# Moving the low-part subtractions of the weights from GpSimd to VectorE, and starting SBUF areas at multiples of 512 bytes

## What is computed

```python
h = rms_norm(x); proj = h @ w_in                      # block 1: pooling + NSA attention
x = x + (gate_pool * y_pool + gate_nsa * y_nsa) @ w_out
h = rms_norm(x); gate_pre, val = split(h @ w_up)      # FFN, conv on the gate
x = x + (silu(causal_dwconv(gate_pre)) * val) @ w_down
h = rmsnorm(x); z = h @ w_in_2                        # block 2: gated delta rule + band attention
q, k, v = silu(causal_dwconv_2(qkv)); oa = gated_delta_rule(q, k, v, g, beta); ob = chunk_band_attention(...)
x = x + (sigmoid(ga) * (oa @ w_branch_a) + sigmoid(gb) * (ob @ w_branch_b)) @ w_out_2
u = causal_dwconv_2(h @ w_up_2) + b                   # FFN, conv on gate and value
x = rmsnorm(x + (silu(gate) * up) @ w_down_2)
```

## Time and profile before

| | us |
|---|---|
| median of 3 runs | 1731.11 (1723.51 to 1732.45) |
| the profiled execution | 1725.94 |
| its span in the trace | 1724.0 |
| busy PE / DVE / POOL / ACT | 1628.1 / 995.8 / 641.3 / 568.8 |

### The profile page before, as it was taken

The page is one execution under the profiler, slowest core; times in us unless marked ns, Lnnn a source line. Parts: engine busy times, 40 slices in busy tenths (PEclk is TensorE's granted clock), DMA queues, the critical chain, the costliest instruction groups (busy, mean ns, idle before and its releaser), DMA issues.

```text
span 1724.0 us, 21757 instructions
## 1 busy us (share of the span) xinstructions
PE 1628.1 (94%) x7872; PEld 1277.9 (74%) x7872; DVE 995.8 (58%) x1295; ACT 568.8 (33%) x906; POOL 641.3 (37%) x274
## 2 busy tenths in 40 slices
PE   6997899999999999999999999999999999998997
PEld 4876666678888887887776798666688777777885
DVE  5146566576777775326924732245566888888223
ACT  5132455544322222223234223135444222222221
POOL 3452211144444444443433541131244444443432
PEclk9998999999999999999999999999999999999998
DMA  6421212142222223222222211252232222223231
GB/s 225 156 87 55 67 56 71 60 161 96 98 97 95 93 96 109 98 83 86 86 92 92 74 38 37 78 208 82 98 137 96 85 85 85 85 85 104 84 101 66
DMA packets 49845, 163.10 MB, mean 95 GB/s; under 512 B 5088, under 2 KB 5352, under 8 KB 49648
## 3 DMA queue, kind: packets, MB, share of 16 engines
q1 hardware_dynamic: 46544, 156.09, 26.4%
q10 hardware_dynamic: 3232, 6.08, 1.0%
HBM read 148.50 MB, written 13.65 MB: 94 GB/s over the span
## 4 chain that ended last, share of the span: by engine, by line
PE 69%; DVE 20%; issue 5%; ACT 4%; DVEq 1%; POOL 0%; DMA 0%; ACTq 0%
PE banks L1452 19%; PE banks L1454 18%; PE banks L1453 18%; DVE t_val L1073 3%; DVE t_gate L1068 3%; DVE cv L1291 2%; DVE t_raw L1012 2%; PE banks L1543 2%; PE banks L1569 2%; PE banks L1552 1%; DVE t_gate L1070 1%; PE banks L1773 1%; PE banks L1762 1%; DVE t_val L1070 1%; DVE t_gate L1089 1%
## 5 line engine op out<-in xcount | busy, mean ns | idle before, releaser
L590 POOL TENSOR_TENSOR w_lo<-w_raw,w_hi 128x1024 fp32r<-128x1024 f32 (+1 forms) x228 | 588.6, 2581 | 1020.8 <-ACT w_hi L679 1020.8
L1452 PE MATMUL banks<-h_hi,w_hi 128*128 128x512 f32 x1312 | 535.8, 408 | 49.6 <-POOL w_lo L590 31.5
L1454 PE MATMUL banks<-h_hi,w_lo 128*128 128x512 f32 x1312 | 514.2, 392 | 0.0
L1453 PE MATMUL banks<-h_lo,w_hi 128*128 128x512 f32 x1312 | 513.8, 392 | 0.0
L679 ACT ACTIVATE w_hi<-w_raw 128x1024 fp32r<-128x1024 f32 (+1 forms) x228 | 250.4, 1098 | 432.4 <-PE banks L1454 397.5
L1452 PEld LDWEIGHTS banks<-h_hi,w_hi 128*128 128x128 f32 x1312 | 247.6, 189 | 127.0 <-issue 53.0
L1454 PEld LDWEIGHTS banks<-h_hi,w_lo 128*128 128x128 f32 x1312 | 247.4, 189 | 53.5
L1453 PEld LDWEIGHTS banks<-h_lo,w_hi 128*128 128x128 f32 x1312 | 247.8, 189 | 51.2 <-issue 4.8
L1452 PE MATMUL banks<-act_hi,w_hi 128*128 128x512 f32 x352 | 140.7, 400 | 4.1 <-DVE t_raw L1012 3.2
L1453 PE MATMUL banks<-act_lo,w_hi 128*128 128x512 f32 x352 | 140.2, 398 | 0.0
L1454 PE MATMUL banks<-act_hi,w_lo 128*128 128x512 f32 x352 | 140.1, 398 | 0.0
(11 more groups left out here) (273 smaller groups left out, 1988.7 us busy)
## 6 DMA issues: line engine op xcount, KB each, us to landing
w_raw<-in_w_up SPq DMA_DIRECT2D x88, 512.0 KB, 3.4
w_raw<-in_w_fill SPq DMA_DIRECT2D x44, 512.0 KB, 3.5
w_raw<-in_w_down SPq DMA_DIRECT2D x32, 704.0 KB, 4.0
late_scratch<-stage SPq DMA_DIRECT2D x44, 256.0 KB, 2.1
w_raw<-in_w_mix SPq DMA_DIRECT2D x16, 512.0 KB, 4.3
sg<-late_scratch SPq DMA_DIRECT2D x16, 512.0 KB, 3.8
w_raw<-in_w_out SPq DMA_DIRECT2D x16, 512.0 KB, 3.5
w_raw<-in_w_in SPq DMA_DIRECT2D x15, 512.0 KB, 3.5
```

Source lines behind the costliest of these rows:

```text
L590: pool.tensor_tensor(w_lo[:, c.slot, 0:kt * P], w_raw[:, c.slot, 0:kt * P], w_hi[:, c.slot, 0:kt * P], ALU.subtract).then_inc(lo_ready, 1)
L1452: pe.matmul(dst, w_h, hi[:, kr, :], start=first and n == 0, stop=False)
L1453: pe.matmul(dst, w_h, lo[:, kr, :], start=False, stop=False)
L1454: mm = pe.matmul(dst, w_l, hi[:, kr, :], start=False, stop=last and n == len(ks) - 1)
```

## The change

POOL keeps the first two low parts and those issued in in1 (up to the first two chunks of fill1). All others, 211 of 228, are formed by DVE with the same instruction. In `ffn` they come right behind each conv, in `residual` for all chunks but the last of the tile before the wait for PE and for the last one behind the tile's work, in `merge` between the sum and `mix_lo`, in in2c behind the taps, in in2z behind the copy. In `late` the low part comes right behind the scaling, but in the steps "unit", "level", "chunk" and "rows" (attention and recurrence) only at the next step ("owed"). DVE waits once for the last low parts of POOL. POOL keeps pooling, memsets and `b_t`. `base` and `arena` are rounded up to 512 bytes instead of 64, so that after it w_hi, h_hi and the arena all start at multiples of 512.

```diff
-        base = -(-nc.sbuf_base // 64) * 64
+        base = -(-nc.sbuf_base // 512) * 512
...
-        arena = at
+        arena = at = -(-at // 512) * 512
...
+        def low(eng, c, kt):
+            eng.wait_ge(hi_ready, c.count(1))
+            eng.tensor_tensor(w_lo[:, c.slot, 0:kt * P], w_raw[:, c.slot, 0:kt * P],
+                              w_hi[:, c.slot, 0:kt * P], ALU.subtract).then_inc(lo_ready, 1)
+        def next_low(eng, name, i, j, q=0):
+            c2, kt2 = ahead(chunk(name, i, j, q), INFO[name][2])
+            if c2:
+                low(eng, c2, kt2)
...
         def _(pool):
-            split("in1")
+            for i, j in units(pool, INFO["in1"][0]):
+                next_low(pool, "in1", i, j)
...
-            serve("norm", 2)
             pooling(pool, 0)
-            serve("norm", 4)
             pooling(pool, 1)
... (every other serve, lows and split of POOL goes)
             def late(name, b, plan, total, stage):
-                state = [0]
+                state, owed = [0], []
+                def settle():
+                    while owed:
+                        n = owed.pop()
+                        next_low(dve, name, n // 2, n % 2)
                 def serve(*at):
                     upto = (plan[at][0] if at else total) // PIECES
+                    settle()
                     while state[0] < upto:
+                        settle()
                         n = state[0]
...
                         state[0] += 1
+                        owed.append(n)
+                    if not at or at[0] not in ("unit", "level", "chunk", "rows"):
+                        settle()
...
             def residual(name, n):
+                    for q in range(per - 1):
+                        next_low(dve, name, i, j, q)
                     dve.wait_ge(chunk_done, chunk(name, i, j, per - 1).count(1))
...
                     gained(n, m, j, isinstance(i, int) and m == 0)
+                    next_low(dve, name, i, j, per - 1)
...
             def merge(name, b, sg, mt, mix_hi, mix_lo):
                     dve.tensor_tensor(mt[:, 2, :], mt[:, 0, :], mt[:, 1, :], ALU.add).then_inc(mixed[b], 1)
+                    next_low(dve, name, i, j)
                     dve.wait_ge(mix_hh[b], lin(j + 1, 2, i))
...
                     conv(t_gate[:, j, :], bank(ACC), t_raw[:, 0, :], f, steps * j, i, j)
+                    next_low(dve, name, i, j, 0)
                     dve.wait_ge(chunk_done, chunk(name, i, j, 1).count(1))
...
                         conv(val, bank(ACC + 1), t_raw[:, 1, :], lin(FK + j, 2, i), steps * j + 4, i, j)
+                    next_low(dve, name, i, j, 1)
                     dve.wait_ge(conv_done[b], lin(steps * j + steps, 2 * steps, i))
...
+            dve.wait_ge(lo_ready, BASE["fill1"] + 2)
             serve = late("fill1", 0, FILL1, FILLED1, stage1)
...
+                next_low(dve, "in2c", i, j)
-            copy_tiles("in2z", p2a[:, 12:17, :])
+            copy_tiles("in2z", p2a[:, 12:17, :], True)
```

More of the change, by code:

```diff
@@ L586, in _ @@
         def _(pool):
[L587 to L601, removed]
-                state = [0]
[L605 to L613, removed]
-            split("in1")
+            low(pool, Chunk(0, 0, 0, None, False), DK)
+            low(pool, Chunk(1, 0, 0, None, False), DK)
+            for i, j in units(pool, INFO["in1"][0]):
+                next_low(pool, "in1", i, j)
             pool.wait_ge(copied["in1"], 15)
@@ L620, in _ @@
             pool.wait_ge(pad_zero, 3)
-            serve = lows("fill1", FILL1, FILLED1)
-            serve("norm", 2)
             pooling(pool, 0)
-            serve("norm", 4)
             pooling(pool, 1)
-            serve("norm", 5)
             pool.wait_ge(n_sum, 6)
             pool.memset(cmp_blk[:, :, :, :, :], 0.0).then_inc(blk_zero, 1)
-            serve("turn", 2)
-            serve("compress", 4)
             pool.wait_ge(c_pe, 2)
             pool.memset(pc_t[:, :, :], 0.0).then_inc(blk_zero, 1)
[L633 to L637, removed]
             pool.wait_ge(copied["in2z"], 5)
             pool.memset(gb_rows[:, :], 0.0).then_inc(blk_zero, 1)
-            serve = lows("fill2", FILL2, FILLED2)
             for h in range(GH):
[L643 to L646, removed]
                 pool.wait_ge(d_dve, 11 * (h + 1) if h < 2 else 11 * GH)
@@ L654, in _ @@
                     .then_inc(i_mask, 1)
[L656 to L664, removed]
             pool.wait_ge(rel_loaded, 16)
             pool.memset(rel[0:CH, :, 0:CH], NEG).then_inc(blk_zero, 1)
-            serve()
-            for name in ("mix2", "out2", "up2", "down2"):
-                split(name)
         @block.scalar
@@ L1034, in residual, with copy_tiles @@
                     gained(n, m, j, isinstance(i, int) and m == 0)
-            def copy_tiles(name, dst):
+                    next_low(dve, name, i, j, per - 1)
+            def copy_tiles(name, dst, lows=False):
                 for i, j in units(dve, INFO[name][0]):
@@ L1039, in copy_tiles @@
                     scaled(dst[:, lin(j, 2, i), :], bank(ACC + j)).then_inc(copied[name], 1)
+                    if lows:
+                        next_low(dve, name, i, j)
             def merge(name, b, sg, mt, mix_hi, mix_lo):
```

## The result

| | us |
|---|---|
| median, changed kernel | 1702.76 (1698.73 to 1704.14) |
| median, kernel before, same chip | 1729.45 (1723.51 to 1732.45) |
| ratio | 0.985, 95% interval 0.981 to 0.988 |
| span of the profiled execution | 1700.8 (before 1724.0) |

Faster by 27 us, about half of the 50 that the prediction's sum gave, and above the upper end of its range (1698). The page of the changed kernel: busy time of each engine, then the group of the low parts (count, busy us, mean ns, idle before it and who ended it).

A forecast was written before the change was run, and what follows sets the result against it. It took PE to bound most stages, and DVE, held up by POOL, to bound up2 and in2c. Terms -23 - 2 - 5 - 6 - 2 - 12 = -50 on 1725.9 gave 1676, written as 1678 us; range 1614 to 1698.

The forecast's parts named there:

- POOL's hold on DVE: In up2, DVE instructions needing what POOL holds stand until POOL is done, losing 3.3 us a tile.
- The two-tile loop of the prediction: In up2, loop from t_raw through low part, PE's chunks and act_lo: 11.12 us a tile; stage 246, -23 us.
- DVE's bare 10.94: DVE's own work per up2 tile, 8.66 us plus 2.28 for two low parts; lower bound for the tile.
- The end of up2: PE stands behind DVE's backlog as up2 ends; an estimated 2 us of that goes.
- in2c: DVE-bound at 5.96 us a chunk; loop through lo_ready gives 5.53, 12 chunks at 0.43 less: -5 us.
- Addresses: Down, mix and out: equal operand offsets give up1's 0.2267 us a matmul everywhere, 6.7 ns less each: -12 us.
- offset 0 better than the rest: Rival: at offset 0 all matmuls run at 0.2133 us, 57 us beyond the forecast, 1621 us; chance 0.34.
- the slower rival: Offset 0 is the worst, 0.240 us a matmul, up2 PE-bound at 11.6 a tile: 1750 us; chance 0.05.
- Attention: 15 low parts fit DVE's waits for the scores while POOL's stalls go: -6 us, bounds +17 and -16.
- Norms, scores and recurrence: Low part comes at once, about +1.2 us at five chunks against stalls that go: -2 us.
- DVE's order costs: Rival: DVE waits head of line behind hi_ready in attention and recurrence, +17 and +8: about 1710 us; chance 0.06.
- The bound of +8: Upper bound on the -2 us term for norms, pooling, compression, scores and recurrence; lower bound -8.

The follow-up runs named there:

- low_behind_mult: Changed kernel with low parts at once in the rows and at the last chunk step, plus feed-forward's second low part behind the gate-value product: 1683.50 us.
- early_low: scores_late with the low part in the feed-forward's convolutions behind the first of three taps, not the third: 1677.51 us, ratio 0.972.
- addr_only: Kernel before with only the two address roundings to 512 bytes, POOL keeping all low parts: 1713.88 us, ratio 0.992.
- all_at_64: Changed kernel with all areas, weights and activations alike, 64 bytes above a multiple of 512: 1697.05 us, ratio 0.981.
- settle_rows: Changed kernel with the owed low part in the recurrence's rows settled at the same step: 1691.24 us, ratio 0.979.
- settle_out: Changed kernel with the low part owed by the recurrence's last chunk step formed there, before the reduction of the squares: 1693.58 us, ratio 0.979.
- scores_late: Changed kernel with low parts at once in rows and last chunk step, plus the fourth compression step's low part behind yp_lo: 1679.00 us, ratio 0.972.

## Why the prediction was right and wrong

**What bounds the kernel, and POOL's hold on DVE: right.** up2 was bound by DVE standing behind POOL. A tile went from 12.19 to 11.23 in the steady part, where intervals of 11.43 and 11.03 alternate. The two-tile loop of the prediction gave 11.12, so it is 0.11 short, and nearer than DVE's bare 10.94; that the mean of all 21 intervals is 11.12 too is luck, as the first and the last are only 10.1 and 10.2. That it is a loop, low_behind_mult and early_low showed: moving DVE's idle time gave 1 us, moving the low part ahead in the loop 4.4. The stage came to 247.2 where 246 was said. The Trainium skill ("SBUF — State Buffer", section "SBUF: two separate sides") has the port shared by DVE and GpSimd as an exclusive lock; the trace agrees, with 319 us of DVE's busy time gone.

**The end of up2: right in kind, mis-sized.** The stall of 3.20 us shrank to 0.78, and the half rate behind it went with it (3.0), 5.4 us in place of 2. addr_only shows that the second part is chance: its stall is 3.17 us at the same place, with the full clock behind it. The 2.4 of the stall are within the 21.1 of the stage in the table, so the tiles themselves gave 18.7 where 23 was said; the two misses nearly cancel.

**in2c: half.** 12 chunks at 5.96 were counted, from one pair of rows; over eleven intervals the kernel before has 5.79 and the changed one 5.55. That this is close to the 5.53 of the loop is partly chance: the changed kernel's intervals alternate between 5.34 and 5.92, which is 5.63, and the first is 4.62. -2.7 instead of -5 (and 1.6 in in2z, where the stretch of 3.4 us at the lower level from 859 is gone): one interval of the middle had been taken for a series whose first two and last are 5.5.

**Addresses: right, value and condition.** 12.1 to 12.6 us for 12, 0.2267 throughout, and equal offsets are enough (all_at_64), though 256 apart does as well. The likeliest rival, offset 0 better than the rest, got 0.34 and is refuted: at 0 the spacing is 0.2267 too. (In the sum of the slower rival, a spacing of 0.240 makes a tile of 48 matmuls 11.5 us and not 11.6, some 2 us less in all; nothing hangs on it.)

**Attention: right in sign.** -5.5 for -6, with DVE's low parts where it waits anyway.

**Norms, scores and recurrence: the step that failed.** The prediction took -2 with bounds -8 and +8, at some 1.2 us a low part, as if each came at its chunk. Measured +23, of which settle_rows gives 10.0 back, settle_out 9.6 and scores_late 4.3, 23.9 in all. It failed in three points. First, it took for "the low part comes at once" what the change defers in the rows: one step late is one step of DVE's list, there a head with eleven instructions and a wait of 2.5 us (9.5 us in all), while PE needs the low part 7 us after the scaling. Second, at the last chunk step it never asked what stands between the owed low part and its settling: a wait for ACT of 7 us and 5.5 us of reduction and scaling. The price of a moved step was taken from its own duration, not from what is in front of it. Third, no term was there for the clock, although the kernel before shows stalls of PE with the lower level behind them. It made 1.7 us of each of the two places in the rows, some 3 before the scores and some 4 at the end of the recurrence, by half of the time at the lower level in which PE was not standing anyway.

The rival "DVE's order costs" came within 8 us of the result with 0.06, but by the wrong wait: it saw DVE stand for w_hi. DVE does wait 96.8 us for w_hi in the changed kernel, but 65 of them in down1 and down2, where it has nothing else to do, and 2.6 in the two attentions together, which gained. With settle_rows DVE stands for w_hi in the rows too, 0.92 us a time, and nothing is lost. The bound of +8 was the error that the range inherited: with it the sum comes to 1688, inside the range's end at 1698, and only a bound of +23 would have held the time.

With the three placements mended the same change gives 1679.0, where the forecast was 1678. That the mends make the difference is shown; the agreement to 1 us is partly luck, since in2c and the tiles of up2 gave less and the clock more.

## What to carry to other kernels

- When work moves from an idle engine to a busy one, price each of its places, not its duration: write down what stands in front of it in the new engine's order, waits included, and when its reader gets there. An instruction put one step later is late by the longest step of the list, and the best place is in front of a wait that is long anyway.
- A stall of TensorE costs more than its length when the clock falls behind it. Look at the granted clock behind the stalls, in the traces of both kernels, before a difference of 2 to 3 us is put down to an edit.
- Idle time inside a loop over several engines is not there to be filled. Find the link that the loop runs through, here the end of the low part, and move that.

## What the runs showed of the hardware

**The clock behind one and the same stall.** Before the scores PE stood 2.82 to 2.87 us in nine kernels. Five of them had 6.8 us at 1.2 GHz from its last microsecond on, one 3.4, three nothing. Windows of the changed kernel and of settle_rows over the same 14 us, with PE's stalls equal to 0.01 us:

```profile
176.00:190.00 14.00, 11.15 (x46) 7.79 (x45) 7.62 (x17) 2.95 (x5) 0.00 (x0) 0.76 0.16 56
```

```profile
176.00:190.00 14.00, 11.16 (x64) 9.13 (x63) 9.60 (x18) 2.27 (x4) 0.00 (x0) 1.00 0.15 56
```

The stall of 6.4 us at the end of the recurrence had 6.8 us at the lower level, beginning 2 to 3 us before its end, in all five kernels that had the stall; the one of 1.7 to 1.8 us before the scores had none in five. Stalls of 1.47 us before mix1 and of 1.42 before mix2's products on oa had 3.4 us behind them in some runs and none in others. So it is a chance that depends on more than the length. The Trainium skill ("TensorE: Matmul & The Clock Gate", section "What's actually happening") says that idleness brings the half rate and that the time at which the chip looks is free-running; the scatter here fits that. It is also a likely part of the spread of a kernel's times, some 5 us here, which no run separated.

**Two operands at unequal offsets.** A matmul of 512 columns takes 226.7 ns where the stationary and the moving operand start at the same place within 512 bytes, or 256 apart, and 232.2 or 233.3 where they are 128 or 64 apart. The Trainium skill (the same page, section "Step-by-step: what each phase is for") says that the loading of weights takes nothing from the running matmul, as the two have read ports of their own; by that rule alone the difference of the addresses should be worth nothing. The runs measure 5.6 and 6.7 ns a matmul at the full clock. Whether it is the loads of weights that cost them, and so whether that rule is wrong, the runs do not show, since every matmul here has its own load. At the lower level the difference is worth nothing: in down2 of the kernel before, with operands 64 bytes apart, ten matmuls at 1.2 GHz take 4.26 us, 0.426 each, the same as the 0.4267 of equal offsets in the earlier trace rows.

```profile
1585.06 0.63 PE L1454 MATMUL banks<-act_hi,w_lo 128*128 128x512 f32 x1
...
1589.32 0.63 PE L1452 MATMUL banks<-act_hi,w_hi 128*128 128x512 f32 x1
```

The 13.3 ns between 226.7 and 512 columns at 2.4 GHz stay unexplained at every offset tried.
